# Expert rows of the last step kept on the chip, planes zeroed early, a closing phase that goes tile by tile

## The reference

```python
def block_ffn(args):
    tok, e = args
    z = h[tok] @ w1[e] + b1[e]
    z_glu, z_lin = jnp.split(z, 2, axis=-1)
    ...
    act = z_glu * jax.nn.sigmoid(SWIGLU_ALPHA * z_glu) * (z_lin + 1.0)
    return act @ w2[e] + b2[e]
...
y = y.reshape(-1, d) * slot_w[:, None].astype(h.dtype)
return jnp.zeros_like(h).at[slot_tok].add(y)
...
h_lat = h_lat + g2 * y.reshape(h_lat.shape)
...
return rmsnorm(h_lat, final_g)
```

## Time and profile before

| | us |
|---|---|
| median of 3 runs | 1590.32 (1587.66 to 1593.16) |
| profiled execution, its own time | 1585.78 |
| its span | 1584.0 |
| TensorE busy | 1461.9 (92%) |
| VectorE busy | 735.8 (46%) |
| ScalarE busy | 261.3 (16%) |
| GpSimd busy | 210.6 (13%) |
| DMA, mean over the span | 314 GB/s |

### The profile page before, as it was taken

One profiled execution on the slowest core, in us unless ns is written; L12 is line 12 of the kernel. 1 busy time (PEld: TensorE's weight loads), 2 busy tenths in 40 slices (PEclk: granted clock), 3 DMA queues, 4 the chain that ended last, 5 costly groups with the idle time before them and its releaser, 6 DMA issues.

```text
span 1584.0 us, 39651 instructions
## 1 busy us (share of the span) xinstructions
PE 1461.9 (92%) x14639; PEld 738.5 (47%) x14639; DVE 735.8 (46%) x2464; ACT 261.3 (16%) x467; POOL 210.6 (13%) x267
## 2 busy tenths in 40 slices
PE   5999999999896899999979999979899979999896
PEld 3658888888653333433323434323333424333232
DVE  4503877777638544443424434424343423434244
ACT  4402555555413200000000000000000000000001
POOL 1000000000051112111211111211121111212110
PEclk9999999999998999999989999979999979999798
DMA  9685211112577999998798999999799998998997
GB/s 388 192 265 148 62 54 53 53 53 57 172 306 274 358 413 407 412 415 347 301 415 339 408 417 417 414 414 417 321 417 416 417 414 321 410 417 344 413 400 295
DMA packets 130857, 497.19 MB, mean 314 GB/s; under 512 B 15356, under 2 KB 48476, under 8 KB 94892
## 3 DMA queue, kind: packets, MB, share of 16 engines
q1 hardware_dynamic: 122396, 479.93, 77.1%
q0 software_dynamic: 8256, 16.81, 2.8%
q10 hardware_dynamic: 176, 0.06, 0.0%
HBM read 484.92 MB, written 17.58 MB: 317 GB/s over the span
## 4 chain that ended last, share of the span: by engine, by line
PE 71%; DMA 15%; SPq 7%; DVE 4%; issue 1%; ACT 1%; ACTq 0%; DVEq 0%; POOLq 0%
PE ps L1838 28%; PE ps L1870 14%; DMA big_b<-in_moe_w 7%; PE ps L1541 6%; PE ps L1542 6%; PE ps L1543 6%; DMA arena<-in_moe_w 5%; SPq L431 4%; PE ps L1720 3%; SPq L425 2%; PE ps L1652 1%; PE ps L1564 1%; DMA arena<-in_final_g 1%; PE ps L1851 1%; PE ps L1666 1%
## 5 line engine op out<-in xcount | busy, mean ns | idle before, releaser
L1838 PE MATMUL ps<-arena,rows 128*32 128x512 f32 x2736 | 318.2, 602 | 26.7 <-DMA arena<-in_moe_w 20.1
L1838 PE MATMUL ps<-big_b,rows 128*32 128x512 f32 x2688 | 316.8, 607 | 21.8 <-DMA big_b<-in_moe_w 21.8
L886 ACT ACTIVATE rows<-ps 128x256 f32<-128x256 f32 x84 | 32.3, 385 | 977.0 <-issue 661.5
L1838 PEld LDWEIGHTS ps<-arena,rows 128*32 128x32 f32 x2736 | 86.8, 111 | 214.0 <-issue 159.2
L1838 PEld LDWEIGHTS ps<-big_b,rows 128*32 128x32 f32 x2688 | 85.5, 111 | 208.1 <-issue 153.3
L1870 PE MATMUL ps<-big_b,rows 128*32 128x256 f32 x2688 | 163.9, 395 | 8.1 <-DMA big_b<-in_moe_w 8.1
L1870 PE MATMUL ps<-arena,rows 128*32 128x256 f32 x2688 | 161.7, 392 | 9.3 <-DMA arena<-in_moe_w 8.5
L1434 DVE SCALAR_TENSOR_TENSOR y_sb<-ps,w_s,g_q 128x256 f32<-128x256 f32 x42 | 20.3, 484 | 261.0 <-PE ps L1870 261.0
L1434 DVE SCALAR_TENSOR_TENSOR rows<-ps,w_s,g_q 128x256 f32<-128x256 f32 x42 | 20.3, 484 | 256.8 <-PE ps L1870 256.8
L1870 PEld LDWEIGHTS ps<-big_b,rows 128*32 128x32 f32 x2688 | 84.2, 113 | 68.1 <-DMA big_b<-in_moe_w 12.9
L1870 PEld LDWEIGHTS ps<-arena,rows 128*32 128x32 f32 x2688 | 84.1, 112 | 67.0 <-DMA arena<-in_moe_w 13.0
(11 more groups left out here) (360 smaller groups left out, 1785.0 us busy)
## 6 DMA issues: line engine op xcount, KB each, us to landing
big_b<-in_moe_w SPq DMA_DIRECT2D x204, 1024.0 KB, 14.2
arena<-in_moe_w SPq DMA_DIRECT2D x180, 1024.0 KB, 15.4
ring_t<-in_hg_w_in SPq DMA_DIRECT2D x32, 512.0 KB, 3.9
ogT<-in_mod_w SPq DMA_DIRECT2D x16, 1024.0 KB, 5.0
arena<-yrows SPq DMA_DIRECT2D x8, 1024.0 KB, 12.6
x_sb<-in_x SPq DMA_DIRECT2D x2, 2048.0 KB, 7.9
arena<-in_hg_w_in SPq DMA_DIRECT2D x4, 1024.0 KB, 13.8
arena<-in_mod_c SPq DMA_DIRECT2D x4, 1024.0 KB, 19.7
```

What stands on the lines that cost most here:

```text
L1838: last = mm(bank[q * G:(q + 1) * G, :], XT[par][:, pos * G:(pos + 1) * G], w[:, :, q * NW:(q + 1) * NW], start=(pos == 0), stop=False)
```

## The change

Before, all steps scatter their rows to `yrows`, and each row of each plane is written once. Now the last step (`par` 1 of the last pair) doesn't scatter.

- *Zeroing.* Since the last step's rows of `yrows` are no longer written, all 2048 rows are first filled with zeros: 16 stores of 128 rows from `slot_io`, which POOL sets to zero at the start. Four stand ahead of the head loop, two in each of its six rounds. POOL waits for them before it writes slot numbers into `slot_io`.
- *The last pair* is written out behind the loops of PE and POOL, which run to `last_pair`. In it PE's last `next_z` and `slots_of` are left out, and POOL's last scatter.
- *A one-hot product.* DVE copies the tokens of the last step aside (`tok_s`), compares them with token numbers from POOL (`tok_io`) into `tok_hot` (128 slots by 512 tokens), and copies the four quarters of y into `y_wide` (128x1024), whose other parts POOL has set to zero. PE adds `tok_hot` times `y_wide` for each tile: two matmuls a tile.
- *Order of the closing phase.* SP issues `hrows` of tile 0, waits for the scatters of the steps before the last, then issues the reads of tile 0, then b2 and g2 as eight loads of 32 partitions and 512 columns, then tile 1, `final_g`, tiles 2 and 3. PE goes tile by tile: `hrows`, one-hot, b2, planes. b2 lies in partition quarters by column half, so that the two b2 matmuls of a tile use two row groups.

The diff, without the lines for names and allocation:

```diff
--- before.py
+++ after.py
@@ -268,8 +269,10 @@
         y_sb = [mv(7), nc.alloc_sbuf_tensor_at("y_sb1", [P, NW], F32, offset=place["res"])[:, :]]
         ygat = arena[:, 0:16384].rearrange("p (i k n) -> p i k n", i=LT, k=TOPK)
         hx = arena[:, 16384:20480].rearrange("p (i n) -> p i n", i=LT)
-        g2_row, fin_row = arena[:, 20480:21504], arena[:, 21504:22528]
-        sq_out, b2_x = arena[:, 22528:23552], arena[:, 23552:24576]
+        b2_h, g2_h, fin_row = arena[:, 20480:20992], arena[:, 20992:21504], arena[:, 21504:22528]
+        sq_out = arena[:, 22528:23552]
+        tok_io, tok_hot = ogT[:, 2, :], ogT[:, 3, :]
+        y_wide = ogT[:, 4:6, :].rearrange("p a n -> p (a n)")
         wd4 = ogT[:, 0, :].rearrange("p (i q e) -> p i q e", i=LT, q=QT)
         wdT = ogT[:, 1, :]
 
@@ -304,11 +308,13 @@
         sec_done = [S["zf_ps"], S["zb_ps"], S["q_ps"], S["g_ps"]]
         ld_mod = [sem(f"ld_mod{s}") for s in range(2)]
         ld_wout = [sem(f"ld_wout{n}") for n in range(2)]
-        ROWS_IN = 32 + 16 * (LT + QT + 2)
         gath = [*ld_wh, *ld_mod, *ld_wout]
         GATHERED = [16 * H + 16] * 4 + [16 * DK + 16] * 2 + [32] * 2
         ld_w1 = [ld_a1, [sem(f"ld_b1_{k}") for k in range(DK)]]
         ld_w2 = [ld_a2, [sem(f"ld_b2_{k}") for k in range(4)]]
+        ld_hx = [S["ld_vec"], S["ld_x"], S["ld_ctx"], S["ld_br"]]
+        HX_IN = (16 * 7, 16 * 3, 16 * 2, 16 * 4)
+        B2_IN, FIN_IN = 32 + 32 * QT, 16 * (3 + QT + 1)
         ld_xg = [sem(f"ld_xg{i}") for i in range(2)]
         y_st = [sem(f"y_st{i}") for i in range(2)]
 
@@ -391,7 +397,18 @@
             for q in range(2):
                 sp.dma_start(n2q[q * QD:(q + 1) * QD, 0:512],
                              norm2_g[q * 512:q * 512 + 512].partition_broadcast(QD)).then_inc(S["ld_mb"], 16)
+            def zero_rows(r0):
+
+                to = yrows[r0:r0 + P, :] if isinstance(r0, int) else yrows[bass.ds(r0, P), :]
+                sp.dma_start(to.rearrange("p (a n) -> p a n", n=P), slot_io[:, :].unsqueeze(1).broadcast_to([P, D // P, P])
+                             ).then_inc(S["zero_st"], 16)
+
+            sp.wait_ge(S["zero_ok"], 1)
+            for n in range(4):
+                zero_rows(n * P)
             with sp.Fori(2, H) as h:
+                for n in range(2):
+                    zero_rows(h * (2 * P) + n * P)
                 for s in range(4):
                     sp.wait_ge(S["whl_ok"], h * 4 + (s - 3))
                     sp.dma_start(wh[:, s], w_in_s[:, :, bass.ds((h - 1) * P + (SEC[s] * D + P), P)]).then_inc(ld_wh[s], 16)
@@ -502,19 +519,26 @@
                             sp.sem_inc(ld_w2[1 - par][k], 16)
                     over_w1(AHEAD, W1C)
 
-            for i in range(LT):
-                sp.dma_start(hx[:, i, :], hrows[i * P:(i + 1) * P, :]).then_inc(S["ld_rw"], 16)
-            for q in range(QT):
-                sp.dma_start(b2_x[q * E:(q + 1) * E, :], moe_b2).then_inc(S["ld_rw"], 16)
-            sp.dma_start(g2_row, mrows[3].partition_broadcast(P)).then_inc(S["ld_rw"], 16)
-            sp.dma_start(fin_row, final_g.partition_broadcast(P)).then_inc(S["ld_rw"], 16)
-            for par in range(2):
-                sp.wait_ge(y_st[par], n_pairs * 16 + 16)
-            for i in range(LT):
+            def rows_back(i):
+
+                sp.dma_start(hx[:, i, :], hrows[i * P:(i + 1) * P, :]).then_inc(ld_hx[i], 16)
+                if i == 0:
+                    for par in range(2):
+                        sp.wait_ge(y_st[par], n_pairs * 16 + (16 - 16 * par))
                 for n in range(2):
                     k = 2 - 2 * n
                     sp.dma_start(ygat[:, i, k:k + 2], yrows.rearrange("(k i p) n -> i p k n", k=TOPK, p=P)[i][:, k:k + 2]
                                  ).then_inc(gath[2 * i + n], 16)
+
+            rows_back(0)
+            for q in range(QT):
+                c0 = (q % 2) * 512
+                sp.dma_start(b2_h[q * E:(q + 1) * E, :], moe_b2[:, c0:c0 + 512]).then_inc(S["ld_rw"], 16)
+                sp.dma_start(g2_h[q * E:(q + 1) * E, :], mrows[3, c0:c0 + 512].partition_broadcast(E)).then_inc(S["ld_rw"], 16)
+            rows_back(1)
+            sp.dma_start(fin_row, final_g.partition_broadcast(P)).then_inc(S["ld_mrow"], 16)
+            for i in range(2, LT):
+                rows_back(i)
             for i in range(LT):
                 sp.wait_ge(S["fin_ok"], i + 1)
                 sp.dma_start(out[i * P:(i + 1) * P, :], ygat[:, i, 0, :]).then_inc(S["out_st"], 16)
@@ -527,6 +551,7 @@
             me.mark(pool.memset(ones[:, :], 1.0))
             me.mark(pool.memset(ident[:, :], 0.0))
             me.mark(pool.memset(mkf, 1.0))
+            pool.memset(slot_io[:, :], 0.0).then_inc(S["zero_ok"], 1)
             me.mark(pool.memset(res[:, :, :], 1.0))
             pool.memset(eps_t[:, :], EPS).then_inc(S["consts"], 1)
             me.wait()
@@ -567,6 +592,7 @@
                     me.link(pool.tensor_copy(bias3[r, :], b_raw[r]))
             pool.sem_inc(S["bias_ok"], 1)
             pool.wait_ge(S["yo_ps"], 6)
+            pool.wait_ge(S["zero_st"], 16 * (TOPK * LAT // P))
             pool.iota(io_e, pattern=[[1, E]], base=0, channel_multiplier=0,
                       allow_small_or_imprecise_dtypes=True).then_inc(S["consts"], 1)
             pool.iota(io_c.rearrange("p (b s) -> p b s", s=2), pattern=[[1, NBT // 2], [4 * E, 2]], base=0,
@@ -639,13 +665,15 @@
             pool.wait_ge(S["idx_ok"], 2)
             gather(1)
 
-            def pair(i):
+            def pair(i, last=False):
 
                 for par in range(2):
                     pool.wait_ge(S["idx_ok"], i * 2 + (par + 3))
                     pool.wait_ge(S["xt_ok"], i * 2 + (par + 1))
                     pool.sem_inc(S["go"], 1)
                     gather(par)
+                    if last and par:
+                        break
                     pool.wait_ge(S["rows_ok"], i * 2 + (par + 1))
                     pool.wait_ge(S["y_ok"], i * 2 + (par + 3))
                     pool.sem_inc(S["go"], 1)
@@ -653,9 +681,15 @@
 
             pair(0)
             pool.wait_ge(S["tab_ok"], 1)
-            n_pairs = pool.value_load(tab_n[0:1, 0:1], min_val=2, max_val=NPAIR_MAX)
-            with pool.Fori(1, n_pairs) as i:
+            last_pair = pool.value_load(tab_n[0:1, 1:2], min_val=1, max_val=NPAIR_MAX - 1)
+            with pool.Fori(1, last_pair) as i:
                 pair(i)
+            pair(last_pair, True)
+            pool.wait_ge(S["w1_used"], last_pair * (2 * W1C) + 2 * W1C)
+            pool.sem_inc(S["go"], 1)
+            pool.memset(y_wide, 0.0).then_inc(S["consts"], 1)
+            pool.iota(tok_io, pattern=[[QT, LAT]], base=0, channel_multiplier=0,
+                      allow_small_or_imprecise_dtypes=True).then_inc(S["consts"], 1)
 
 
         @block.scalar
@@ -1371,6 +1405,8 @@
                 dve.wait_ge(y_st[par], i * 16 + 16)
                 V.tensor_copy(row_s[par][:, :], row_n[par][:, :]).then_inc(S["rows_ok"], 1)
                 me.mark(V.tensor_copy(w_s[par][:, :], w_n[par][:, :]))
+                if par:
+                    me.mark(V.tensor_copy(tok_s[:, :], tok_n[1][:, :]))
 
             dve.wait_ge(S["tab_ps"], 6)
             for par in range(2):
@@ -1393,7 +1429,9 @@
             me.mark(V.scalar_tensor_tensor(end_c, by_rank[:, 0:1], 1.0, at_2[:, 1:2], ALU.mult, ALU.add))
             me.link(V.tensor_scalar(past[0:E], io_c[0:E], at_2[:, 1:2], None, ALU.is_ge))
             V.scalar_tensor_tensor(ind16, io_c[0:E], end_c, past[0:E], ALU.is_lt, ALU.mult).then_inc(S["row_ok"], 1)
-            me.mark(V.tensor_scalar(tab_n[:, 0:1], so_far[0:1, E:E + 1], lead[0:1, E:E + 1], 0.5, ALU.add, ALU.mult))
+            me.link(V.tensor_scalar(tab_nn[:, 0:1], so_far[0:1, E:E + 1], lead[0:1, E:E + 1], 0.5, ALU.add, ALU.mult))
+            me.mark(V.tensor_copy(tab_n[:, 0:1], tab_nn[:, 0:1]))
+            me.mark(V.tensor_scalar(tab_n[:, 1:2], tab_nn[:, 0:1], 1.0, None, ALU.subtract))
             dve.wait_ge(S["row_ok"], 5)
             me.mark(V.memset(tab_nf[:, 0:2], 0.0))
 
@@ -1471,8 +1509,18 @@
             w_part = lambda n: kw16[:, :, n, 0:E].unsqueeze(2).broadcast_to([P, LT, QT, E])
             me.link(V.tensor_tensor(wd4, w_part(1), w_part(2), ALU.add))
             V.tensor_tensor(wd4, wd4, w_part(3), ALU.add).then_inc(S["b2_ok"], 1)
-            dve.wait_ge(S["ld_rw"], ROWS_IN)
-            V.tensor_tensor(b2_x, b2_x, g2_row, ALU.mult).then_inc(S["b2_ok"], 1)
+            me.link(V.tensor_tensor(tok_s[:, :], tok_s[:, :], q_col[:, :], ALU.subtract))
+            dve.wait_ge(S["y_ok"], n_pairs * 2 + 2)
+            dve.wait_ge(S["consts"], N_CONST + 2)
+            me.mark(V.tensor_scalar(tok_hot, tok_io, tok_s[:, :], None, ALU.is_equal))
+            for q in range(QT):
+                r = slice(q * G, (q + 1) * G)
+                me.mark(V.tensor_copy(y_wide[r, q * NW:(q + 1) * NW], y_sb[1][r, :]))
+            me.wait()
+            dve.sem_inc(S["b2_ok"], 1)
```

(43 more changed lines are left out.)

6 lines of the change are left out of this document (4 added, 2 removed).

## The result

| | before | after |
|---|---|---|
| median of the runs | 1590.18 us (1584.63 to 1598.48, 20 runs) | 1596.76 us (1587.88 to 1602.65, 20 runs) |
| profiled execution, its own time / span | 1585.78 / 1584.0 us | 1598.37 / 1596.6 us |
| time as a share of before, 95% interval | | 1.0037 (1.0023 to 1.0051) |
| start of the tail, T | 1532.42 us | 1540.03 us |
| tail, T to end of the span | 51.6 us | 56.6 us |

The changed kernel is slower, by 0.37% or 5.9 us, with an interval of 3.7 to 8.1 us (the two medians lie 6.6 us apart). The forecast was 2.3 us more, 1592.6 us; 1596.8 lies inside the range and outside of what was called likeliest.

The account below looks back on a forecast made before the run. TensorE was taken to bind the closing phase: the reads start 13.4 us earlier, but 9.1 us of added matmuls and a 4.3 us b2 wait move the end from 1584.0 to 1586.3. 1590.3 + 2.3 = 1592.6 us, range 1587 to 1598.

Parts of the forecast that it names:

- The mechanism of the forecast: Closing phase: yrows reads start 13.4 us earlier, but TensorE's added 9.1 us eat that; end 2.3 us later, chance 0.68.
- The product's eight matmuls: Closing phase, TensorE: two full one-hot matmuls for each of four tiles, 0.875 us each, 7.0 us added.
- The wait for b2: Tile 0: TensorE waits 4.3 us for b2 times g2, whose loads are queued behind the first yrows reads.
- rival B: Closing phase: reads of yrows set the end; up to 13.4 us earlier, about 8 with slow loads, 1582 us; chance 0.07.
- rival D: Closing phase: the scatter before the last lands late, reads start after 1541; +4 to +6 us, 1595 us; chance 0.06.
- rival E: Heads: the zero stores use up the 33.7 us lead and delay a head's weights; 1593 us and more; chance 0.02.
- the removed `next_z`: End of the last step: TensorE's 24 needless matmuls, 5.33 us, go; y comes at 1540.4 instead of 1541.8, 1.4 us left.
- the clock: Closing phase: TensorE's two pauses lower its clock for a while; 1.0 us taken, between 0 and 3.4.
- Rival C: Closing phase: bursts between waits keep TensorE at its lower clock; +4.8 us, with late b2 +6.5, 1597 us; chance 0.17.
- the signs of being right: Tail: y at 1540-1542, yrows reads near 1537, 4 us b2 wait, 28-30 us run, last matmul within 4 of 1576.4.
- the bound of 0.3%: Whole kernel: 4.8 us, what a measurement can tell from no change; slower by more 0.21, within 0.71.
- the routing table and the steps: Ahead of the tail: table operations some 0.4 us, priced 0, at most 0.3; one 128x1 copy per pair, priced 0.

Follow-up runs that it names:

- e3_no_hot: The changed kernel without its eight one-hot matmuls, so the last step's rows are missing from the output; tail 53.3 us, ratio to before 1.0018.
- e1_zero_only: The kernel before with only the 16 stores that zero yrows, and the wait for them, added; tail 52.1 us, ratio to before 1.0007.
- f1_peel_only: The kernel before without the last next_z, the last small slot product and the bias product behind the loop; tail 52.6 us, ratio to before 1.0011.
- f2: The changed kernel with 24 matmuls of 512 columns, result unused, ahead of the last second product; tail 52.8 us, ratio to before 1.0031.
- f4: The changed kernel with b2 and g2 loaded ahead of the first yrows reads, plane 2 on DVE and 24 unused matmuls; tail 49.0 us, ratio 0.9997.
- e2: The changed kernel with the eight b2 and g2 loads issued before SP waits for the scatters; tail 55.3 us, ratio to before 1.0028.
- e4: The changed kernel with plane 2 of yrows added by DVE instead of TensorE; tail 49.9 us, ratio to before 1.0009.
- f3: The changed kernel with b2 and g2 loaded behind SP's wait but ahead of the first yrows reads, and plane 2 on DVE; tail 49.0 us, ratio 0.9992.

## Why the prediction was right or wrong, point by point

All positions count from T of the respective profile.

| step | forecast | after | before |
|---|---|---|---|
| reads of `yrows` issued | +5.0 | +4.95 | +18.4 |
| last weight piece used | +6.6 | +7.7 | |
| y scaled | +8.0 | +9.3 | +9.4 |
| one-hot tile and y copies done | +12.3 | +12.5 | |
| `hrows` and one-hot of tile 0 done | +13.6 | +16.3 | |
| first b2 matmul | +17.9 | +18.9 | |
| first four planes take | 3.5 | 5.4 | |
| one tile | 7.9 | 8.1 | |
| last matmul | +47.1 | +49.8 | +43.9 |
| from there to the end | 6.8 | 6.8 | 7.6 |
| tail | 53.9 | 56.6 | 51.6 |

*Right.* The mechanism of the forecast: reads 13.4 us earlier, no gain, because TensorE's tail becomes longer. The product's eight matmuls were priced at 7.0 us, two of them hidden ahead of the wait for b2; taking them out shortened each of the three later tiles by 1.71 us, 5.1 us in all (e3_no_hot). The wait for b2 stands where it was expected, 2.6 us long instead of 4.3, since tile 0's first matmuls ended 2.7 us later than forecast, in part at the lower clock. The reads are hidden (last stretch: DMA 0.31), so rival B falls. The reads went out at T+4.95, so rival D falls. Zeroing costs nothing measurable and no head's weights come late (e1_zero_only), so rival E falls, although its price was wrong: the 3.9 us of the earlier trace rows stood for a store that took 6.3 us to land and 1.39 us of SP to issue.

*Wrong, the removed `next_z`.* I gave it 1.4 us: the last weight piece by its landing, then a quarter and the scaling. It gave nothing: y at T+9.3 against T+9.4, and the same in f1_peel_only. What failed is the position of the last piece: T+7.7 instead of the T+6.6 that the landing of the earlier trace rows had led me to set, 1.1 of the 1.3 us. The second product does begin early, but has to go at the pace of its weights, in pieces at a clock of 0.74 and 0.80, where a quarter takes 1.93 us instead of 0.91; that slow quarter doesn't set y, since a wait of 0.59 us for the last piece stands behind it. Before, the removed matmuls had filled this time, the weights had all arrived, and 3.66 us of product ran in one go. Whether the removal itself made the last piece late isn't shown, but the profiles side with it: it landed at T+5.9 to T+6.7 in the four with matmuls in this place (before, e1, f2, f4), at T+7.0 to T+7.8 in five without, and at T+10.0 in e2. Work whose result was thrown away was useful in that it cost no time and kept the clock up.

*Mis-sized, the tail.* Forecast +2.3 us, measured +5.0 us. Of the 2.7 us, 1.05 come before the first b2 matmul (T+18.9 for T+17.9, b2 and g2 landed at T+18.1 for T+17.2), and 1.6 between it and the last matmul: 0.8 us in the last three tiles (24.5 for 23.7), and 0.8 us in tile 0. There 6.3 us pass from the first b2 matmul to the next tile where 4.5 were forecast (the four planes took 5.40 for 3.5), 1.8 us more, and only 1.0 us of a possible 3.4 had been set aside for the clock. Rival C had named this: less than its price, since from 1565.26 on every group runs at full speed again and the clock of the last stretch is 1.00, but in its direction. The Trainium skill, page "TensorE: Matmul & The Clock Gate", section "HAM oscillation", says that gaps in TensorE's work put the clock back to 1.2 GHz. The trace agrees for the start of the tail (0.73 to 0.80 with the gaps, 1.00 with the filler). That the lower clock would last through the tail, as rival C feared, did not happen here. C's price for the worst case, 6.5 us, was also more than its own terms give: 4.8 us, and 0.8 us for the late b2, are 5.6.

*Signs.* Of the signs of being right, counted from T, y and the reads came where they were named, but the wait was 2.6 us and not some 4, the run behind it 30.8 us and not 28 to 30, and the last matmul came 5.8 us later (T+49.8 for T+43.9) and not within 4. That is again the two small terms, and not another mechanism.

*Chances.* With a measured ratio of 1.0037 the time is just beyond the bound of 0.3% that I gave 0.21; the interval, 1.0023 to 1.0051, doesn't exclude the side that I gave 0.71. From the forecast's 2.3 us to the bound of 4.8 us were 2.5 us, and the two small terms of the tail, 1.05 and 1.6 us, together use them up.

*Open: the time ahead of T.* In the two profiles T differs by 7.6 us. One stretch of some 105 us, from SP's first loads for the router to its first store of `frows`, shows of what kind a large part of this is (columns as above). Before:

```profile
380.04:485.12 105.08, 100.04 (x554) 66.20 (x555) 64.52 (x119) 34.85 (x61) 28.32 (x42) 1.00 0.62 225
```

after:

```profile
379.29:487.67 108.38, 103.30 (x554) 68.31 (x554) 68.17 (x119) 34.83 (x61) 28.70 (x42) 0.97 0.60 218
```

e1_zero_only, which shares only the zeroing with it:

```profile
379.23:487.51 108.28, 103.26 (x554) 68.29 (x554) 68.11 (x119) 34.84 (x61) 28.70 (x42) 0.97 0.60 219
```

e2_b2_first, which has the whole change:

```profile
381.18:486.31 105.13, 100.08 (x554) 66.23 (x555) 65.58 (x119) 34.83 (x61) 28.36 (x42) 1.00 0.62 225
```

The same work takes 105.1 us at a granted clock of 1.00 and 108.3 us at 0.97. In all ten profiles there are three values: 105.1 (before, f1, e2), 108.0 to 108.4 at 0.97 (the changed kernel, e1, e3, f2) and 109.9 to 110.7 at 0.95 (e4, f3, f4). They part behind a wait of TensorE for DVE that all ten have at the same place, 3.56 or 3.57 us long; the 12 records of L1720 (L1768 in the changed kernel) behind it take 5.32 us in the three quick ones, 7.0 us in the middle four, 7.8 or 7.9 us in the slowest three. In the changed kernel:

```profile
426.15 0.66 PE L1723 MATMUL ps<-ident,rows 128*128 128x128 f32 x4 [3.56 <-DVE rows L1107]
426.65 7.01 PE L1768 MATMUL ps<-ring_t,ogT 128*128 128x512 f32 x12
```

The change doesn't force the slow value, since e2_b2_first has all of it and the quick one. Whether it makes it more likely is open: both kernels without the zero stores are quick, and only one of the eight with them. It is 3.3 of the 7.6 us; from there to T the difference is 5.1 us more over 1050 us, less 0.8 us by which the changed kernel was ahead at 379.29. The profiled execution of before was besides 4.4 us under its median. So the 12.6 us between the spans are no measure of the change.

But the tails don't explain all of it either. The ratio of each kernel, times 1590 us, is more than the difference of its tail to 51.6 us: by 0.9 us for the changed kernel, 0.6 to 1.3 for e1, e2, e3, f1 and f3, and 2.1, 3.2 and 3.7 for f4, e4 and f2. Each of these has an interval of some 3 us to either side, and all share the one tail of before, so that a cost of a microsecond or two ahead of the tail is neither shown nor excluded. There is a hint of it: from the first store of `frows` to T the seven profiles with the whole change take 1049.3 to 1053.8 us, the three without it (before, e1, f1) 1047.3 to 1049.6. There lie the routing table and the steps, which the forecast priced at 0. No experiment here isolates it.

**The best version.** f3_mid_plane2 is 0.9992 of the kernel before (0.9970 to 1.0014), 0.45% under the changed kernel's 1.0037, and still not measurably faster than the kernel before. Its bound is the order of the loads: `final_g` stands ahead of DVE's first sum. Whether a later place of that wait would bring the missing 2.3 us wasn't tried.

## What to carry to other kernels

A transfer that is started 13 us earlier gains only what the engine behind it has to spare; before the change TensorE was full for the 24.5 us up to its last matmul, and the sum had to be made on that engine, where 9 us came in. Before work is removed in front of a wait for data, ask whether that work was hidden by the wait: here 5.3 us came off and y was ready at the same moment, at a lower clock. Moving a small load ahead in a full queue can move something else back, as in e2_b2_first, so look at what is already on its way. And when a wait goes away, look where the time came from: in e2_b2_first all of the gain, in f3_mid_plane2 half of TensorE's, was the clock behind the wait.

## What the runs showed of the hardware that was not expected

- Matmuls whose result is thrown away can shorten the stretch that follows: with 24 more of them the granted clock from 1545 to 1559 is 1.00 instead of 0.74 and 0.87, and the tail in the profile 52.8 us instead of 56.6 (1.7 us of it clock, 2.1 us a landing that isn't explained). The times of the whole kernel don't resolve it.
- The upper clock stayed in that tail in spite of TensorE's waits of 2.03 and 2.26 us; in e3_no_hot, with a wait of 6.42 us, it was 1.00 before and 0.50 behind it, and a b2 pair took 2.08 instead of 1.13 us. In the changed kernel, which has no filler, it was 0.74 behind a wait of 2.38 us.
- Behind the same wait of 3.56 us, at a place where the kernels have the same matmuls, the clock stayed up in three profiles and fell in seven: 12 records took 5.32, 7.0 or 7.8 us, and the whole stretch 3 or 5 us more. Two profiles can so differ by more than the whole effect of this change.
- With eight loads of 32 partitions issued 13 to 16 us behind it, the data of a weight load of 1 MB was used 2.3 us later (T+9.98 for T+7.67); the full DMA engines moved 228 GB/s in the last 5 us of that wait, and the first of the small loads landed before it. This is one profile.
- A store of 512 KB in pieces of 512 B from one source that is read again and again took 6.3 us to land and 1.39 us of SP to issue, where a load of the same size and pieces took 3.9 us.
